# Remainders of five weight units made by adding DMAs instead of VectorE

## What is computed

```python
h2 = rmsnorm(x, norm_mlp_g[l])
x = x + jnp.square(jax.nn.relu(h2 @ w_up[l])) @ w_down[l]     # D_FF = 4096, w_down 4096 x 1024
...
return rmsnorm(x, norm_final_g)
```

## Time and profile before

| what | value |
|---|---|
| runs | 902.76, 902.78, 904.44 us; median 902.78 |
| profiled execution | 903.25 us, its span 901.5 us |
| TensorE busy | 889.1 us (99%) |
| VectorE busy | 665.6 us (74%) |
| ScalarE busy | 482.4 us (54%) |
| GpSimd busy | 53.6 us (6%) |
| DMA | 163.89 MB, mean 182 GB/s, all but 0.78 MB of it on the queue q1 |

### The profile page before, as it was taken

How to read it: one execution, slowest core, us unless ns; L and a number is a source line. 1 busy time by engine, 2 the same in 40 slices (tenths; PEclk the granted TensorE clock), 3 DMA queues, 4 the chain that set the end, 5 groups by cost and what they waited for, 6 DMA issues and landing times. The chain is left out here.

```text
span 901.5 us, 12223 instructions
## 1 busy us (share of the span) xinstructions
PE 889.1 (99%) x4931; PEld 760.0 (84%) x4931; DVE 665.6 (74%) x725; ACT 482.4 (54%) x556; POOL 53.6 (6%) x78
## 2 busy tenths in 40 slices
PE   8999999999999999999999999999999999999997
PEld 7988888788778788888888888889987888888886
DVE  5766668767557556676788888887796789877996
ACT  6434444445555445445555555456777765555552
POOL 1110000002312101000000000001000010000000
PEclk9999999999999999999999999999999999999999
DMA  9655555584453534465465556636943476666561
GB/s 303 218 162 182 191 194 183 183 298 130 169 180 121 179 130 153 172 195 203 163 200 191 192 174 206 215 110 194 280 141 95 136 238 187 187 188 208 166 210 47
DMA packets 98572, 163.89 MB, mean 182 GB/s; under 512 B 5271, under 2 KB 37799, under 8 KB 98388
## 3 DMA queue, kind: packets, MB, share of 16 engines
q1 hardware_dynamic: 98516, 163.11, 55.5%
HBM read 162.04 MB, written 3.16 MB: 183 GB/s over the span
## 5 line engine op out<-in xcount | busy, mean ns | idle before, releaser
L1709 DVE TENSOR_TENSOR wlo<-land,whi 128x2048 fp32r<-128x2048 f32 (+2 forms) x142 | 311.9, 2201 | 66.5 <-ACT whi L1248 66.1
L1248 ACT ACTIVATE whi<-land 128x2048 fp32r<-128x2048 f32 (+1 forms) x142 | 261.0, 1843 | 110.9 <-PE acc L630 43.8
L678 PE MATMUL m<-xT,whi 128*128 128x512 f32 x480 | 114.5, 391 | 0.0
L678 PE MATMUL acc<-xT,whi 128*128 128x512 f32 x448 | 107.7, 391 | 0.2 <-DVE gu L2452 0.2
L678 PEld LDWEIGHTS m<-xT,whi 128*128 128x128 f32 x480 | 88.2, 188 | 17.0
L678 PEld LDWEIGHTS acc<-xT,whi 128*128 128x128 f32 x448 | 82.2, 188 | 16.2 <-DVE gu L2452 0.4
L628 PE MATMUL acc<-whi,xT 128*128 128x512 f32 (+2 forms) x240 | 92.5, 386 | 2.0 <-issue 2.0
L629 PE MATMUL acc<-wlo,xT 128*128 128x512 f32 (+2 forms) x240 | 90.3, 376 | 0.0
L630 PE MATMUL acc<-whi,xT 128*128 128x512 f32 (+2 forms) x240 | 90.2, 376 | 0.0
L683 PEld LDWEIGHTS m<-xT,wlo 128*128 128x128 f32 x480 | 61.5, 191 | 2.3
L683 PE MATMUL m<-xT,wlo 128*128 128x256 f32 x480 | 62.3, 283 | 0.0
(11 more groups left out here) (489 smaller groups left out, 1516.7 us busy)
## 6 DMA issues: line engine op xcount, KB each, us to landing
land<-in_w_in SPq DMA_DIRECT2D x55, 1024.0 KB, 5.2
land<-in_w_up SPq DMA_DIRECT2D x16, 1024.0 KB, 5.4
land<-in_w_ffn_gate SPq DMA_DIRECT2D x22, 512.0 KB, 4.0
land<-in_w_ffn_up SPq DMA_DIRECT2D x22, 512.0 KB, 5.1
land<-in_w_down SPq DMA_DIRECT2D x18, 512.0 KB, 4.6
land<-in_w_in SPq DMA_DIRECT2D x14, 512.0 KB, 4.8
land<-in_w_out SPq DMA_DIRECT2D x6, 1024.0 KB, 5.1
land<-in_w_ffn_down SPq DMA_DIRECT2D x6, 1024.0 KB, 5.2
```

Of the source, the lines that this page charges most:

```text
L678: mm(to[:, c, :], whi[:, s, k, c * P:(c + 1) * P], xT[:, k0 + k].rearrange("p a t -> p (a t)"), start=k0 + k == 0, stop=False, skip_group_ ...
L1248: activate(whi[:, u % PARTS, 0:m, 0:w], land[:, u % LANDS, 0:m, 0:w], ACT.Copy).then_inc(hi_ready, 1)
L1709: v.tensor_tensor(wlo[:, u % PARTS, 0:m, 0:w], land[:, u % LANDS, 0:m, 0:w], whi[:, u % PARTS, 0:m, 0:w].bitcast(F32), ALU.subtract).then_ ...
```

## The change

Five plain units of the first down product, those with a pair on either side (`BY_DMA`: 87, 89, 91, 93 and 95), get their `wlo` in another way. VectorE skips them. ScalarE writes the negated rounded weight into `wlo` in two halves (`minus`, a copy with scale -1 to fp32r), and for each half GpSimd issues a DMA that adds the landed weight onto it: `-hi + weight`, the same remainder. GpSimd's ten DMAs stand in its program between the inverse root ahead of the up product and the one behind the down product. A unit's readiness is now a semaphore of its land slot, `lo_added`, of which the two DMAs of a unit bring 32; for other units `lo_ready` counts on without the five. SyncE's load into that land buffer waits for `lo_added` and, new, for `hi_ready`.

```diff
--- before.py
+++ after.py
@@ -171,6 +171,7 @@
 UNITS[_at:] = [(G_AT["dn0"], 0, 0) if c == "S" else _rest[c].pop(0) for c in "1S0S0S0S1011"]
 PAIR_AT = {_u: _i for _i, _u in enumerate(u for u, unit in enumerate(UNITS) if unit[2] == 0)}
 PAIR_U = list(PAIR_AT)
+BY_DMA = [_u for _u, _unit in enumerate(UNITS) if GROUPS[_unit[0]][0][:4] == "down" and _u - 1 in PAIR_AT and _u + 1 in PAIR_AT]
 FIRST_U, LAST_U = {}, {}
 for _u, (_n, _k, _m) in enumerate(UNITS):
     FIRST_U.setdefault(GROUPS[_n][0], _u)
@@ -203,6 +204,11 @@
 def whole(name):
 
     return name in BY_TURNS or name[:2] == "up" or name[:2] == "gu" and name != "gu0"
+
+
+def lo_count(u):
+
+    return sum(v not in BY_DMA for v in range(u + 1))
 
 
 def reads_before(n, eng):
@@ -409,6 +415,8 @@
     half_hi, half_lo = sem("half_hi"), sem("half_lo")
     half_out, conv_made = sem("half_out"), sem("conv_made")
     hi_ready, lo_ready, units_done = sem("hi_ready"), sem("lo_ready"), sem("units_done")
+    minus_ready = sem("minus_ready")
+    lo_added = [sem(f"lo_added{i}") for i in range(LANDS)]
     read_act, read_dve = sem("read_act"), sem("read_dve")
     turned, turn_hi, turn_lo = sem("turned"), sem("turn_hi"), sem("turn_lo")
     tile_done = sem("tile_done")
@@ -464,6 +472,13 @@
 
     SUMMED = [f"up{i}" for i in range(PAIRS)] + [f"gu{i}" for i in range(PAIRS2)]
     SUM_AT = {LAST_U[name]: i for i, name in enumerate(SUMMED)}
+    def wait_rest(eng, u):
+
+        if u in BY_DMA:
+            eng.wait_ge(lo_added[u % LANDS], 32 * sum(v <= u and v % LANDS == u % LANDS for v in BY_DMA))
+        else:
+            eng.wait_ge(lo_ready, lo_count(u))
+
     block = ctx.enter_context(nc.Block())
 
 
@@ -478,7 +493,9 @@
             n, k, m = UNITS[u]
             _, weight, segs, *_ = GROUPS[n]
             if u >= LANDS:
-                sp.wait_ge(lo_ready, u - LANDS + 1)
+                wait_rest(sp, u - LANDS)
+                if u - LANDS in BY_DMA:
+                    sp.wait_ge(hi_ready, u - LANDS + 1)
             at = 0
             if u == 0:
                 (col, w), = segs
@@ -615,7 +632,7 @@
                 group_read(n - 2)
             for k in range(m):
                 if k == 0:
-                    pe.wait_ge(lo_ready, u + 1)
+                    wait_rest(pe, u)
                 first, end = k0 + k == 0, k0 + k == kk - 1
                 if k > 0:
                     between(u, k)
@@ -1247,6 +1264,13 @@
                 return
             activate(whi[:, u % PARTS, 0:m, 0:w], land[:, u % LANDS, 0:m, 0:w], ACT.Copy).then_inc(hi_ready, 1)
 
+        def minus(u):
+
+            act.wait_ge(landed[u % LANDS], land_count(u))
+            act.wait_ge(units_done, u - PARTS + 1)
+            for ks in (slice(0, UK // 2), slice(UK // 2, UK)):
+                activate(wlo[:, u % PARTS, ks, :], land[:, u % LANDS, ks, :], ACT.Copy, scale=-1.0).then_inc(minus_ready, 1)
+
         def square(j, src, junk, halves):
 
             for t in range(TT):
@@ -1513,6 +1537,8 @@
                 lru_sigmoids()
             if u == B2 + 9:
                 gla_copies()
+            if u + 2 in BY_DMA:
+                minus(u + 2)
             if u + 1 in PAIR_AT:
                 wsum_leading(PAIR_AT[u + 1])
             if u == PAIR_U[PAIRS - 1] + 1:
@@ -1704,6 +1730,8 @@
             if u in PAIR_AT:
                 pair_split(u)
                 return
+            if u in BY_DMA:
+                return
             dve.wait_ge(hi_ready, u + 1)
             dve.wait_ge(landed[u % LANDS], land_count(u))
             v.tensor_tensor(wlo[:, u % PARTS, 0:m, 0:w], land[:, u % LANDS, 0:m, 0:w],
@@ -2522,6 +2550,11 @@
                                mhalf[:].to_broadcast([P, TT * ML_H]), ALU.pow), ml_rs)
         inverse_root(1, [(sq_act, 2), (sq_act, 3)])
         signal(g.tensor_tensor(up_scale[:, :], rstd[:, 1, :], rstd[:, 1, :], ALU.mult), up_scaled)
+        for i, u in enumerate(BY_DMA):
+            for half, ks in enumerate((slice(0, UK // 2), slice(UK // 2, UK))):
+                pool.wait_ge(minus_ready, 2 * i + half + 1)
+                g.dma_start(wlo[:, u % PARTS, ks, :], land[:, u % LANDS, ks, :], accum_op=ALU.add).then_inc(
+                    lo_added[u % LANDS], 16)
         inverse_root(2, [(sq_act, 4), (sq_act, 6)])
 
         pool.wait_ge(sq_act, 7)
```

## The result

The changed kernel takes 917.07 us (median of 4 runs, 914.63 to 917.87); beside it the kernel before took 902.77 (902.64 to 904.44). The ratio is 1.0147 [1.0134, 1.0159]: slower. That is 14.3 us more, where 3.9 were forecast (906.7, slower, in a range of 902.0 to 919.3): the direction was right, the size was not. The profiled execution took 916.94 us, 13.7 more than that of before.

The account below looks back on a forecast made before the run. TensorE, busy throughout the first down product, was taken as the bound. VectorE's and ScalarE's changes counted 0, late adds 3.9 us, making the median 906.7 from 902.78; range 902.0 to 919.3.

Parts of the forecast that it names:

- VectorE's and ScalarE's terms: First down product: VectorE loses five subtractions, 11.4 us; ScalarE gains negated copies, 9.5 us; both worth 0 in time.
- a sign against itself: Gaps of TensorE inside the pairs, before the weight sums, would mean ScalarE's place in the order was the cost.
- The price of the add: Engine time A of adding one 1.05 MB unit by DMA: taken as 3.95 us, bounds 3.16 and 6.32.
- The rival built on two reads: Add's time goes by bytes fetched: A 6.32, 16.5 us lost, median 919.3; chance 0.18, shared with slow descriptors.
- Even sharing: Two DMA queues share the engines evenly, so an add takes 2A as long as loads are there.
- the prediction's sum: Lateness of units 87 to 95: 6A - 19.8 while load 89 outlasts the first add; 3.9 us at A = 3.95.
- The negated copy's wait on landing: ScalarE's negated copy needs its unit landed, and weight sums queue behind it; costed at 0, load 93 landing 3.8 us ahead.
- such a ring: Loads, copies and adds each waiting for the one before, once A passes about 5; part of a case of 16.5 us.
- Large and small by turns: TensorE's gaps ahead of the first matmul of units 87 to 95 alternate: 0.3, 1.5, 0.3, 1.5, 0.3 us.
- The engines' share in 535 to 580: Share of the DMA engines in that stretch of the down product, expected above 0.9 if the forecast was right.
- The cover rival: Adds served ahead of the loads, or A under 3.6, keep the loss below 1.8 us: 902.8 us; chance 0.38.

Follow-up runs that it names:

- the adds first: Changed kernel, but SyncE holds the load of unit u + 2 until GpSimd has issued the adds of unit u: 915.81 us, 1.0135; with half units 903.92, 1.0002.
- the run with small loads: Changed kernel with the loads of weight-pair units 88 to 96 cut to 0.19 MB each: 914.86 us, 1.0120.
- The runs with zero products: Changed kernel, with TensorE multiplying a zeroed operand 5, 16 and 12 times ahead of its waits in units 87, 89, 93: 916.20 us, 1.0145.

## Why the prediction was right in sign and wrong in size

- **VectorE's and ScalarE's terms hold.** Forecast 11.4 less and 9.5 more, measured 10.4 less and 9.3 more; both cost 0 by themselves (VectorE's additions in place of the DMA: 0.9996). Only where loads come late does ScalarE's new place cost something: 0.37 us inside pair 88, and 2.2 in four pairs with the adds first. The prediction had named such gaps as a sign against itself; they are the smaller part.
- **The price of the add was the step that failed.** I took A = 3.95 us of all engines for a unit, "on the load's side of the bounds, since the load is the only bulk transfer with a row". It is 5.9 by the queue's share, near the upper bound of 6.32. At full engines a load moves 0.40 MB per us, GpSimd's plain copy 0.39, the add 0.19 (rows at the end of the experiments). So an add takes about twice a load's time, and GpSimd's issuing isn't what slows it. The Trainium skill, Collectives: The Full Stack, The bandwidth ceiling: the fold count and why AG ≠ RS ≠ AR, gives 1.93 times for the adding step of a collective against a plain copy, and puts it down to the second source read; 0.40 / 0.19 = 2.1 and 5.9 / 3.16 = 1.9 agree with the ratio. No run here tells a second read from the addition itself. The rival built on two reads, with 6.32 and a time of 912 and up, had about the right price. It had 0.18; it should have had the most.
- **Even sharing failed too, and a right total would have been luck.** At A = 5.9 load 89 ends before the first add, so the prediction's sum is (A - 2.94) + 2 (2A - 6.1) = 14.4 us, which would make 917.2, nearly the measured 917.07. But its parts are others: 3.0 for every other unit and 2.7 for those between, against 8.7 us of waits, in large and small ones, and 3.3 of clock. It lets an add beside loads take 2A and one alone A. Measured, adds alone for 3 us, adds idle for 4 us, then mixed, with three quarters of the engines for the add: what is issued first mostly goes first. The Trainium skill, DMA: Bandwidth & Descriptors, Queues, rings and completion order, has each engine go round its queues packet by packet; the mixed stretches can be read so (130 and 148 packets of q0 and q1 in 544 to 548 with adds first, at 76.7% and 22.0% of the engines, so even by packets and not by time), the stretches with no byte of an issued add can't. The order alone was worth 5.4 us with half units, 4.2 with plain copies and 1.1 (1.0147 to 1.0135, within the intervals) with whole units.
- **The negated copy's wait on landing was costed at 0.** I looked at load 93 and found 3.8 us of cover. The first one to run out was load 89: behind the adds of 87 it landed 9.7 us after its issue, and its copy was 2.9 us late (539.74 against 536.9); the copies of 91 and 93 were 1.5 and 0.7 late. That puts load and add in series. With the adds first that chain sets the period; in the changed kernel it is one part of the lateness beside the adds' wait behind loads. I had named such a ring only as a rival's consequence, for A above 5.
- **Large and small by turns: right.** 1.4, 4.5, 0, 2.9, 0 (without the clock) against 0.3, 1.5, 0.3, 1.5, 0.3: a late unit gives the next add its time. The engines' share in 535 to 580, forecast above 0.9, is 0.92; the run with small loads, as slow at 0.80, says that this is not what costs.
- **The clock wasn't in the sum.** It took 3.3 us in the profiled run (1.74 + 1.53). The runs with zero products suggest that most of it lies in time that the adds take anyway.
- **The cover rival** falls with A: it needed A under 3.6, or adds served ahead of the loads. With the adds first and half a unit's bytes it came true (1.0002); with the adds first alone it didn't (1.0135).

What stays open: in the changed kernel's own order, how the 12 us divide between the add's length and the loads ahead of it. Taking the addition away gave back 8.3 us, taking the pairs' loads almost away 2, and the order alone 1; with the order, half the add's bytes gave back nearly all. The parts don't add up one by one, since each lateness gives the next add time.

## What to carry to other kernels

Before handing a subtraction to a DMA, lay the whole chain on one line (the copy that prepares it, issue, the add at twice a load's time, the load that ends up behind it) and compare it with the time between two uses, since an engine with spare share doesn't help a chain that is too long. Decide by hand which transfer is issued first: the one whose reader comes first. And where the profile has no row for an operation that reads two streams, don't lean to the nearest transfer that happens to have a row: here the price by the streams read (6.32) was close to the 5.9 measured, and the one near a load (3.95) was not.

## What the runs showed of the hardware that I had not expected

- An add from SBUF to SBUF by DMA moved 0.19 MB per us with the 16 engines at 109%; a plain copy issued in the same way 0.39 at 106%, a load 0.40 at 105%.
- GpSimd takes 0.86 us to issue an add of 512 KB and 0.54 for a plain copy, SyncE mostly 0.4 to 0.5 for a load.
- GpSimd stood idle for 4.7 to 8.8 us ahead of the second of two DMAs, three times in the run with adds between idle buffers, and in every unit when the adds read from HBM; the profile shows nothing that it waited for.
- Adds that had been issued moved no byte for about 4 us while earlier loads were under way (1.6 on idle engines), and a load moved almost none for 3 us while earlier adds were; later both mixed.
- TensorE's granted clock fell behind idle times of 3.54 and 2.73 us (with plain copies, behind one of 1.87), and stayed at 1.00 through nine of 0.4 to 1.6 us with adds first.
